# Six weight buffers moved apart by small unused tiles in a two-layer hybrid encoder kernel

## What is computed

```python
n = rms_norm(h, norm_mix[l]); p = n @ w_in[l]            # columns parted among three mixers
h = h + concat(latent_attention(p), gated_linear(p), hgrn2(p)) @ w_mix_out[l]
h = h + cross_attention(rms_norm(h), rms_norm(mem))      # 4 heads, 256 memory tokens
gate, up = split(rms_norm(h) @ w_ffn_in[l])              # width 2816 each
h = h + (silu(causal_conv3(gate)) * up) @ w_ffn_out[l]
```

## Time and profile before

| | us |
|---|---|
| median of 3 runs | 1418.03 |
| lowest, highest | 1417.41, 1419.02 |
| span of the profiled execution | 1418.1 |

### The profile page before, as it was taken

One profiled execution on the slowest core, in us unless ns is written; L12 is line 12 of the kernel. 1 busy time (PEld: TensorE's weight loads), 2 busy tenths in 40 slices (PEclk: granted clock), 3 DMA queues, 4 the chain that ended last, 5 costly groups with the idle time before them and its releaser, 6 DMA issues.

```text
span 1418.1 us, 17472 instructions
## 1 busy us (share of the span) xinstructions
PE 1400.8 (99%) x6863; PEld 1149.9 (81%) x6863; DVE 766.2 (54%) x1120; ACT 621.9 (44%) x1080; POOL 666.8 (47%) x371
## 2 busy tenths in 40 slices
PE   8999999999999999999999999999999999999999
PEld 6888778887788888888888887788778888888887
DVE  5574675565776305663165655836657652066611
ACT  6747482755433212333346555735753322132321
POOL 5635654552444444444346367535344444444443
PEclk9999999999999999999999999999999999999999
DMA  6332002331233323333333220223223333333322
GB/s 181 94 97 72 18 23 88 115 106 58 76 117 90 102 91 104 104 89 97 97 90 102 86 60 15 75 68 112 89 67 97 104 89 97 100 97 97 100 91 87
DMA packets 176305, 125.67 MB, mean 89 GB/s; under 512 B 14657, under 2 KB 152672, under 8 KB 176224
## 3 DMA queue, kind: packets, MB, share of 16 engines
q1 hardware_dynamic: 175664, 124.55, 29.5%
q10 hardware_dynamic: 560, 0.01, 0.0%
HBM read 122.44 MB, written 2.10 MB: 88 GB/s over the span
## 4 chain that ended last, share of the span: by engine, by line
PE 95%; DVE 2%; issue 1%; ACT 1%; DMA 1%; SPq 0%; DVEq 0%
PE bank L639 28%; PE bank L643 28%; PE bank L641 28%; PE bank L813 2%; PE bank L942 1%; PE bank L943 1%; PE bank L801 1%; PE bank L1022 1%; PE bank L982 1%; DVE Q L1831 1%; PE bank L1097 1%; DVE scores_h L1863 1%; PE bank L921 1%; DMA x_tok<-in_x 1%; DVE scores_g L1863 1%
## 5 line engine op out<-in xcount | busy, mean ns | idle before, releaser
L565 POOL TENSOR_TENSOR w_lo<-raw,w_hi 128x1024 fp32r<-128x1024 f32 (+2 forms) x230 | 545.9, 2377 | 664.8 <-ACT w_hi L1173 663.2
L1173 ACT ACTIVATE w_hi<-raw 128x1024 fp32r<-128x1024 f32 (+3 forms) x229 | 236.5, 1035 | 331.0 <-PE bank L643 330.6
L639 PE MATMUL bank<-x_hi,w_hi 128*128 128x512 f32 x944 | 371.4, 393 | 3.3 <-issue 1.6
L643 PE MATMUL bank<-x_hi,w_lo 128*128 128x512 f32 x944 | 367.5, 389 | 0.0
L641 PE MATMUL bank<-x_lo,w_hi 128*128 128x512 f32 x944 | 367.4, 389 | 0.0
L639 PEld LDWEIGHTS bank<-x_hi,w_hi 128*128 128x128 f32 x944 | 177.2, 188 | 46.1 <-issue 6.5
L641 PEld LDWEIGHTS bank<-x_lo,w_hi 128*128 128x128 f32 x944 | 177.2, 188 | 37.4 <-issue 1.4
L643 PEld LDWEIGHTS bank<-x_hi,w_lo 128*128 128x128 f32 x944 | 177.2, 188 | 37.3
L1950 DVE SCALAR_TENSOR_TENSOR conv<-gate_in,gains_all,conv 128x512 f32<-128x512 f32 x44 | 118.1, 2685 | 1.6
L1537 ACT ACTIVATE conv_silu<-conv 128x512 f32<-128x512 f32 x44 | 27.8, 632 | 169.5 <-DVE conv L1951 169.5
L1673 DVE TENSOR_TENSOR h<-h,bank 128x512 f32<-128x512 f32 x48 | 31.8, 681 | 105.2 <-PE bank L643 105.1
(11 more groups left out here) (318 smaller groups left out, 2276.2 us busy)
## 6 DMA issues: line engine op xcount, KB each, us to landing
raw<-in_w_ffn_in SPq DMA_DIRECT2D x88, 512.0 KB, 3.8
raw<-in_w_ffn_out SPq DMA_DIRECT2D x40, 512.0 KB, 3.6
raw<-in_w_in SPq DMA_DIRECT2D x27, 512.0 KB, 3.8
raw<-in_w_mix_out SPq DMA_DIRECT2D x16, 512.0 KB, 3.9
raw<-in_w_ca_kv SPq DMA_DIRECT2D x32, 256.0 KB, 3.2
raw<-in_w_ca_q SPq DMA_DIRECT2D x8, 512.0 KB, 3.4
raw<-in_w_ca_out SPq DMA_DIRECT2D x8, 512.0 KB, 3.8
raw<-in_w_in SPq DMA_DIRECT2D x12, 256.0 KB, 2.9
```

The lines of the kernel that those rows point to most:

```text
L565: pool.tensor_tensor(w_lo[gi % SPLIT][:, c0:n], raw[gi % RAW][:, c0:n], w_hi[gi % SPLIT][:, c0:n].bitcast(f32), ALU.subtract).then_inc(S[" ...
L639: pe.matmul(o, ah, bh, start=first, stop=False)
L643: mm = pe.matmul(o, al, bh, start=False, stop=last)
L1173: act_.activation(w_hi[k % SPLIT][:, 0:n], raw[k % RAW][:, 0:n], ACT.Copy).then_inc(S["hi_split"], 1)
```

## The change

A tile that nothing reads or writes is reserved behind each of the six buffers, of 4, 4, 8, 8, 8 and 32 float32 elements. No other line is changed, and the instructions of every engine stay the same in kind, number and order; only addresses differ.

```diff
-        w_hi = [sb(f"w_hi{i}", [P, SLAB], f32r) for i in range(SPLIT)]
-        w_lo = [sb(f"w_lo{i}", [P, SLAB], f32r) for i in range(SPLIT)]
+        w_hi, w_lo = [], []
+        for tiles, kind, skews in ((w_hi, "w_hi", (4, 4, 8)), (w_lo, "w_lo", (8, 8, 32))):
+            for i, skew in enumerate(skews):
+                tiles.append(sb(f"{kind}{i}", [P, SLAB], f32r))
+                sb(f"skew_{kind}{i}", [P, skew])
```

## The result

The changed kernel takes 1438.63 us (median of 4 runs, 1438.47 to 1441.03), the kernel before 1417.72 us beside it (4 runs, 1416.71 to 1419.02). The ratio is 1.0146, with a 95% interval of 1.0132 to 1.0161: 20.9 us slower. The prediction was 1418.0 us, no change, with a range up to 1423.3 us; the time lies 15 us above that range.

What follows compares the result with a forecast made beforehand. TensorE's pass spacing was taken as the bound. Span 1418.1 us plus zero for TensorE, other engines and DMAs gave a median of 1418.0 us, no change (0.81), range 1416.0 to 1423.3 us.

Steps and rivals of the forecast that it cites:

- What bounds the kernel: TensorE, busy 1400.8 of 1418.1 us: only the spacing of its split-operand passes, or a wait of TensorE, moves the end.
- Its own sign of a wrong reason: Pass spacing on TensorE moving by over half a nanosecond would show the reason wrong, even where the sum hides it.
- Step (a): TensorE's 5232 split-operand passes at shifted addresses: zero cost, at most 1 ns a pass or 5.2 us.
- Step (b): ScalarE, GpSimd and VectorE at shifted addresses: zero cost, 0.05 us either way from two stalls on GpSimd's splits.
- Step (c): DMAs landing in the moved arena: zero cost, up to 0.2 us on TensorE's 2.0 us wait for input.
- its estimate on the beats of a row: DMA of a 4096-byte row: wasted 32-byte beats go from 4 to 5 beside its 128, under 1%.
- The sum: Whole kernel: span 1418.1 us plus zero for TensorE, GpSimd and input, giving 1418.1 us, 1418.0 us as a median.
- The ragged start: Rival on TensorE: operands starting 32 bytes past a 64-byte boundary lengthen each pass; 1 ns gives 1423.3 us; chance 0.14.
- The eased collision: Rival on TensorE: skewed starts keep weight load and streamed read from meeting; 1348 us, a tenth gives 1411; chance 0.05.
- The weight path: Rival: GpSimd or ScalarE losing a tenth per split gives 1418.6 us, inside no change; part of the forecast's case.
- The granted clock: Rival: same dips to half clock expected; one short dip more or less moves the time 1.7 us either way.
- By buffer: Sign in TensorE's timeline: a spacing change would differ by split buffer, passes on unmoved w_hi0 against those on w_lo2.

Runs made afterwards that it cites:

- e5: Separate program, matmuls alone with other engines idle, streamed tile at chosen distances from the stationary one: float32r 512-column passes 226.67 ns at distance 0, 233.32 at 32 bytes.
- e3: Kernel before with a 32-byte unused tile ahead of raw0, so raw, split buffers and everything behind move together to 160: 1417.31 us, ratio 0.9996.
- e9: Kernel before with only the three w_lo buffers moved to 160, all else still at 128: 1444.71 us, ratio 1.0187.
- m_third: Part of a matmul-only program: every third pass uses a stationary tile at an uneven distance, the others distance 0; 231.5, 232.7 and 233.5 ns by position.
- e13: Matmul-only program, five distances each begun clean, behind five passes 32 bytes apart, or behind five 464-column passes: distance 0 always settles at 226.67 ns.
- e10: Kernel before with everything behind the six split buffers moved by 64 bytes, the buffers unmoved: 1433.12 us, ratio 1.0102.
- e12: Kernel before with each slab placed so the streamed operand begins 16 bytes ahead of the stationary one's place (distance 240): 1442.98 us, ratio 1.0171.
- e1: Kernel before with everything behind the six split buffers moved by 32 bytes, the buffers unmoved: 1448.03 us, ratio 1.0208.
- e11: Second matmul-only program, further distances and mixtures of stationary tiles: 240 bytes 226.67 ns a pass; 8, 48, 192, 224 and 288 bytes 233.3 ns.
- e7: Kernel before with everything behind the six split buffers moved by 256 bytes, the buffers unmoved: 1418.66 us, ratio 1.0006.

## Why the prediction was wrong, point by point

**What bounds the kernel** was right: only the spacing of the passes or a wait of TensorE could move the end, and it was the spacing. Its own sign of a wrong reason, a spacing moved by over half a nanosecond, is what happened; it moved by 4.7.

**Step (a), the term of TensorE, is the one that failed.** It was put at 0 with an upper bound of 1 ns a pass, 5.2 us. It measured 4.72 ns on some 4770 passes, 22.5 us. The bound came from the earlier trace rows, a pair of stretches with 464 columns and a shift of 64 bytes, and was carried over to 512 columns and other shifts. e5 shows that this pair is blind: at 464 columns the passes are at 210.0 ns with either distance, even at distance 0 eight cycles more over their columns than 512 or 384 columns have. The prediction had itself noted that the 464-column passes have 2 ns more over their length than the 512-column ones and had put that down to the length alone; it was the sign that the two are not in the same regime. A bound from the nearest row holds only as far as the row is in the same regime.

**The trace of before had the price in it.** The 370 or so distances off 226 and 227 ns, most of them between 224 and 236 ns, behind stalls and other matmuls show how the same passes go when the rhythm is not there. Their mean, 231 ns at 370 us, is close to that of the changed kernel. I had read the spacing in one settled stretch of 15 passes and not its distribution over the trace. Even so, that the addresses were what held the rhythm could not be read there.

**Step (b), other engines**, held in sum. The split moved by 4 ns (2397 to 2401), L1253 by none. One part was off: the rotary tables went from 459 to 483 ns, where "different places cost GpSimd nothing" had been read. These are 16 operations in the trace and cost TensorE nothing that can be seen. **Step (c), DMAs**, held: 0.2 us, its upper end. No run tests its estimate on the beats of a row.

**The sum.** Besides (a) it set the profiled span equal to the median. In all runs here the span is 1.8 us below the time of the same execution, so the profiled execution of before was 1.9 us longer than the median one. That is not what made the prediction miss.

**The rivals.** The ragged start had the right engine, sign and kind of size (it named 1 ns, and the spacing would have had to be five times that), but its mechanism is refuted by e3: all operands at a ragged place cost nothing. The eased collision looked at the right quantity, the places of the two reads against each other, and had the sign the wrong way round: equal places are the good case. Its counter-argument from the Trainium skill ("SBUF — State Buffer", "Who interferes with whom"), that the two reads have ports of their own, would leave no dependence of one read on the place of the other; the measurement decides against that conclusion for float32r passes of 512 columns (226.7 against 233.3 ns in e5, with all other engines at rest), whatever the two share. The weight path stayed covered. The granted clock did not keep its places: the dip that is missing is the long one, which gave back 3.4 us, where the prediction had allowed for a short one of 1.7.

**What was to show it.** "By buffer" did not come true: in the second layer's feed-forward part, where the weights are stationary, slabs in `w_hi0` and `w_lo0` average 231.1 ns a pass, in `w_hi1` and `w_lo1` 232.6 and in `w_hi2` and `w_lo2` 231.4. The activations behind the buffers have moved as well, so that it is `w_hi1` and not `w_hi0` that lies at their place, 160; and its slabs are the slowest. That fits e9 and `m_third`, where one pass in three at another distance spoils the others; here it is the one on `w_lo1`.

**What stays open.** Why equal places let the passes fall into the rhythm, and what the two reads share, no run here tells. Nor does any tell why the rhythm at other places depends on the start (240: 226.67, 233.33 or 236.67 ns), or why 64 bytes on is 228.9 ns from four starts in e5 and e13 but 228.9 or 233.3 by turns in the kernel (e10, a mean of 231.5 where the weights are stationary). So the cost at another distance could be measured here but not foretold; that distance 0 is fast held in every run. That the start also makes the runs of one slow variant differ more than those of before (e12: 1439.9 to 1447.1 us) fits this, but wasn't tested. No variant was faster than the kernel before.

## What to carry to other kernels

Where TensorE is the bound with float32r passes of 512 columns, keep the tiles it streams and the tiles it holds at the same place modulo 256 bytes, and print the addresses after any new tile: 32 bytes reserved between them cost this kernel 2.1% (e1) and 1.9% (e9), 256 bytes nothing. When an edit only moves addresses, look at the distribution of the start-to-start distances over the whole trace and not at one stretch. And before a bound is taken from a row of another shape, ask whether the two shapes behave alike, for instance whether they have the same time over their columns; a small program with the passes alone, some 30 us for each case, answers that directly.

## What the runs showed of the hardware

- A float32r pass of 512 columns takes 226.67 ns in the rhythm, which at 2.4 GHz is 544 cycles, 32 more than its columns; out of it 228.9 to 236.7 ns. bf16 passes of the same size take 215.8 ns and each of the two records of a float32 matmul 429.2 ns, at any distance tried.
- Where the granted clock is at half, 1.2 GHz, a pass takes 427 ns, 512 cycles with nothing over. In the kernel before (a stretch with PE, PEld, DVE, ACT and POOL, then the granted clock; two lines of the timeline of PE):

```profile
143.40:145.00 1.60, 1.60 (x5) 1.27 (x4) 1.56 (x5) 0.91 (x3) 0.00 (x0) 0.50 0.00 0
...
143.35 0.63 PE L641 MATMUL bank<-w_lo,x_hi 128*128 128x512 f32 x1
...
145.06 0.48 PE L643 MATMUL bank<-w_hi,x_lo 128*128 128x512 f32 x1
```

  From one to the other four passes begin, 1.71 us / 4 = 427 ns. The first passes of e5, behind 15 us in which TensorE did nothing, are 427 ns apart as well, though the row of their granted clock says 1.00; why, no run here shows.
- The rhythm takes up to ten passes to form at distance 0, and one pass in three at another distance (32 bytes in e9, 160 in `m_third`) is enough to keep it from forming.
- At 240 bytes the same passes run in one of three rhythms (226.67, 233.33 or 236.67 ns; e11, e12, e13) and at 64 bytes in one of two (228.9 or 233.3 ns; e10), and hold it over long stretches.
- It is the distance between the two operands that counts, modulo 256 bytes (e5, e7); not their absolute place (e3, all at 160 instead of 128). The other engines have no part in it that shows: e5 has it with all of them at rest.
